# Gated attention: the norm's root moved ahead of evictions on ScalarE; delta net: four fill steps fewer in a head

## What is computed

```python
def gated_deltanet(h, w_in, conv_w, ...):
    proj = h @ w_in                                   # q, k, v, z (the gate), b, a
    qkv = silu(causal_depthwise_conv(proj[..., :3 * DN_WIDTH], conv_w))   # 4 taps
    q, k = l2_normalize(q), l2_normalize(k)           # each head
    o = chunk_gated_delta_rule(q, k, v, beta, g)      # chunks of 64, triangular solve
    o = o * rsqrt(mean(o * o) + EPS) * norm_w * silu(z)
    return o @ w_out

def readout(o_f, o_b, g):                             # the gated linear attention's end
    o = rmsnorm(o_f + flip(o_b), gain)                # mean of squares over a head, its root
    return o * silu(g)
```

## Time and profile before

| | |
|---|---|
| median of three runs | 3222.49 us |
| profiled execution | 3223.74 us |
| its span | 3222.0 us |
| TensorE busy | 3057.1 us, 95% |
| VectorE busy | 1556.7 us, 48% |
| ScalarE busy | 997.9 us, 31% |
| delta net's heads | from about 128 to 745 us |
| gated linear attention | from about 2000 to 2389 us |
| mean granted clock of TensorE | 0.982 |

### The profile page before, as it was taken

How to read it: one execution, slowest core, us unless ns; L and a number is a source line. 1 busy time by engine, 2 the same in 40 slices (tenths; PEclk the granted TensorE clock), 3 DMA queues, 4 the chain that set the end, 5 groups by cost and what they waited for, 6 DMA issues and landing times.

```text
span 3222.0 us, 36124 instructions
## 1 busy us (share of the span) xinstructions
PE 3057.1 (95%) x14927; PEld 2493.4 (77%) x14927; DVE 1556.7 (48%) x1915; ACT 997.9 (31%) x1440; POOL 450.8 (14%) x352
## 2 busy tenths in 40 slices
PE   7899999989899999999979999999998999999997
PEld 5688888878688888888765667888876888888886
DVE  7566666653565553433456773466654222222224
ACT  5555555552211122212333332233232211111111
POOL 4333333321000001001300000233310000000001
PEclk9999999999999999999989999999999999999999
DMA  3111111122133431111220001011131111111111
GB/s 123 40 47 47 46 47 46 47 66 98 59 118 118 128 117 57 47 52 46 92 54 5 9 9 44 20 40 34 53 107 31 52 53 46 46 52 46 46 46 59
DMA packets 77236, 184.76 MB, mean 57 GB/s; under 512 B 7056, under 2 KB 29072, under 8 KB 77072
## 3 DMA queue, kind: packets, MB, share of 16 engines
q1 hardware_dynamic: 77072, 182.44, 17.9%
HBM read 163.87 MB, written 15.79 MB: 56 GB/s over the span
## 4 chain that ended last, share of the span: by engine, by line
PE 85%; DVE 8%; ACT 4%; issue 2%; DMA 0%; POOL 0%; SPq 0%; POOLq 0%; DVEq 0%; ACTq 0%
PE ps L512 38%; PE ps L1561 18%; PE ps L2886 9%; PE ps L2227 4%; DVE b L2835 2%; PE ps L2365 1%; PE ps L2195 1%; PE ps L909 1%; PE ps L2220 1%; PE ps L2219 1%; DVE b L501 1%; ACT b L493 1%; PE ps L916 1%; PE ps L86 1%; PE ps L891 1%
## 5 line engine op out<-in xcount | busy, mean ns | idle before, releaser
L512 PE MATMUL ps<-b 128*128 128x512 f32 x6024 | 1498.5, 400 | 40.1 <-DVE b L501 13.6
L512 PEld LDWEIGHTS ps<-b 128*128 128x128 f32 x6024 | 1111.2, 190 | 258.2 <-issue 19.2
L1561 PE MATMUL ps<-b 128*128 128x512 f32 x2592 | 599.1, 392 | 0.7 <-DVE b L1696 0.7
L1561 PEld LDWEIGHTS ps<-b 128*128 128x128 f32 x2592 | 485.1, 188 | 109.2 <-DVE b L1696 1.1
L501 DVE TENSOR_TENSOR b<-b 128x1024 fp32r<-128x1024 f32 (+1 forms) x206 | 255.4, 1241 | 298.8 <-ACT b L493 291.9
L493 ACT ACTIVATE b<-b 128x1024 fp32r<-128x1024 f32 (+1 forms) x206 | 215.1, 1045 | 524.5 <-PE ps L1561 427.6
L2886 PE MATMUL ps<-b 128*128 128x512 f32 (+1 forms) x1464 | 330.1, 381 | 6.8 <-ACT b L2946 5.9
L2886 PEld LDWEIGHTS ps<-b 128*128 128x128 f32 x1464 | 257.1, 193 | 57.0 <-issue 11.6
L1610 ACT ACTIVATE b<-ps 128x1024 f32<-128x1024 f32 x54 | 55.4, 1026 | 378.4 <-PE ps L512 378.4
L1400 POOL TENSOR_TENSOR b<-b 128x1024 f32<-128x1024 f32 x18 | 43.2, 2399 | 915.5 <-ACT b L1431 915.1
L2227 PE MATMUL ps<-b 128*128 128x512 f32 x320 | 162.9, 592 | 0.0
(11 more groups left out here) (304 smaller groups left out, 3287.9 us busy)
## 6 DMA issues: line engine op xcount, KB each, us to landing
b<-in_down SPq DMA_DIRECT2D x52, 512.0 KB, 3.6
b<-in_mod SPq DMA_DIRECT2D x96, 256.0 KB, 2.6
b<-in_gu SPq DMA_DIRECT2D x44, 512.0 KB, 3.6
b<-scratch SPq DMA_DIRECT2D x38, 512.0 KB, 4.4
b<-in_dn_in SPq DMA_DIRECT2D x32, 512.0 KB, 4.9
b<-in_up SPq DMA_DIRECT2D x32, 512.0 KB, 3.7
b<-in_win SPq DMA_DIRECT2D x26, 512.0 KB, 3.7
scratch<-b SPq DMA_DIRECT2D x18, 512.0 KB, 2.9
```

Of the source, the lines that this page charges most:

```text
L512: ins = e.matmul(ps[:, c], w, h[:, k, c], start=first and k == 0 and i == 0, stop=last and k == KT - 1 and i == 2)
L1561: ins = e.matmul(ps[:, c], w, u[:, at[k], c], start=k == 0 and p == 0, stop=k == n - 1 and p == 2)
```

## The change

In the delta net's half generators of TensorE, ScalarE and VectorE, the number of fill steps behind product "a" becomes 1 + f in levels 1 and 2 only, and 1 in levels 3 to 6. So a head takes four steps fewer, and what of the projections is not done goes on in the next head. In the gated linear attention ScalarE's six fill steps go from ahead of `act_roots` to behind the root.

```diff
@@ pe_delta_half, act_delta_half, dve_delta_half
-            yield 1 + f
+            yield 1 + (f if lv < 3 else 0)
@@ act_gla
             e.activation(B["sq"], B["qf"], ACT.Square).then_inc(*A.up("osq", h))
-            side.fill(self.gla_fill(h, 6))
             self.act_roots(e, A)
             e.wait_ge(*V.at("oms", h))
             e.activation(small[:, 8:16], small[:, 0:8], ACT.Sqrt).then_inc(*A.up("ort", h))
+            side.fill(self.gla_fill(h, 6))
             side.until((h, "g"))
```

## The result

The changed kernel takes 3234.64 us (median of six runs, 3230.99 to 3237.13), the kernel before 3223.12 us beside it (3222.05 to 3225.54): ratio 1.0032, 95% interval 1.0021 to 1.0042. So it is about 11 us slower, where I forecast 13.5 us faster; the time lies outside my range. The profiled execution took 3234.0 us with a span of 3232.2, 10.2 us more than the span before.

What follows compares the result with a forecast made beforehand. TensorE was taken as nearly full in middle heads, idle in the last head and at the attention's root waits. Gains of 11.5 and 3.5 minus 1.5 us made 13.5, so 3222.49 became 3209.0 us; range 3202 to 3216.

Steps and rivals of the forecast that it cites:

- Part 1, the mechanism: Gated attention, first three heads: moving the root ends TensorE's wait of L79 for L2587, 7.6 us, without delaying the evictions.
- Part 1, the size: Gated attention: 7.6 us of waits, 0.5 us for the gate's eviction and 3.4 us of clock, 11.5 us gained, at least 7.6.
- the term for the clock: Gated attention: half-clock stretches right after the first and third heads' stalls vanish, gaining 3.4 us, bounds 0 to 3.4.
- Part 2, heads 0 to 6: Delta net, four fill steps fewer a head: net loss 1.5 us over seven heads, from 2 us gain to 6 us loss.
- That 0.45 us are enough where VectorE is free, and 0.7 us a head is the price where it has taps.: Delta net levels 3 to 6: one short step costs nothing or some 0.1 us; one tap run costs 0.7 us a head.
- That the last two steps are empty.: Delta net: a head has 66 steps but a projection only 64, so the last two were taken as empty.
- That the lag costs nothing but the last head.: Delta net: two steps of lag a head push the last gate's 12 steps, 8.2 us, into head 7; SyncE cost nothing.
- Part 2, the last head: Delta net, head 7: 12.4 us of waits and low clock become 8.9 us, a gain of 3.5 us.
- (a): Last delta-net head, preparation: v's last taps and Silu run there too; 2.0 us of wait, bounds 0 to 3.4.
- (b): Last delta-net head: mixing starts behind the gate's eviction on ScalarE; 5.5 us of wait, bounds 2 to 9, no clock drop.
- (c): Last delta-net head, end: the wait for L1343 is covered, but the sixth tile's piece waits about as much, 1.4 us.
- the one on the other side: Rival, 3%: VectorE bounds the delta net's levels; 28 shortened levels wait 0.68 us each, part 2 costs 18 us, 3229 us.

Runs made afterwards that it cites:

- the root alone: Against the kernel before, only ScalarE's six fill steps in the gated linear attention moved behind the root, delta net unchanged: 3218.69 us, ratio 0.9979.
- the delta net's part alone: Against the kernel before, only the four fill steps fewer a head in levels 3 to 6, attention unchanged: 3239.43 us, ratio 1.0055.
- level 3's kernel: Against the kernel before, one fill step moved from level 3 to the end of the half, so no lag: 3229.69 us, ratio 1.0018.
- the kernel with the gate's unit finished early: Against the kernel before, two steps fewer a head (levels 5 and 6), gate's eviction issued in the projection's last step: 3229.62 us, ratio 1.0018.
- The kernel with full levels and the same lag: Against the changed kernel, the four steps a head taken from the head's end instead of the levels: 3239.94 us, ratio 1.0054 against the kernel before.

## Why the prediction was wrong, point by point

**Part 1, the mechanism: right.** The first attention head's end after the change, ScalarE, VectorE, TensorE:

```profile
2102.96 0.21 ACT L2466 ACTIVATE b<-b 128x8 f32<-128x8 f32 x1 [2.27 <-DVE b L2585]
2103.18 1.28 ACT L2929 ACT_TABLE_LOAD   x1
...
2105.29 1.28 ACT L2929 ACTIVATE b<-ps 128x512 f32<-128x512 f32 x2 [0.82 <-PE ps L2886]
...
2103.20 0.20 DVE L2587 RECIPROCAL b<-b 128x8 f32<-128x8 f32 x1 [0.28 <-ACT b L2466]
2105.77 1.03 PE L79 MATMUL ps<-b 128*128 128x128 f32 x8
```

The root ends 0.2 us behind the mean, the reciprocal 2.4 us ahead of L79, and L79 has no wait. The Silu table is back 0.8 us before the product of the eviction, so the evictions are not late. The three waits' 7.6 us are gone as forecast, and the 0.55 us for the gate's eviction too. This also answers the sentence on the Trainium skill's page "ScalarE: Activation LUTs", section "What ACT_TABLE_LOAD costs": with its drain of about 1380 ns behind the load the eviction would have begun at 2105.8, and it began at 2105.29, when its product came. The row decides.

**Part 1, the size: the term for the clock failed.** I took 3.4 us as a full gain, by the two low stretches directly behind the waits. Those two are gone, but others came: the fourth head had one of 3.4 us, from 2345.1, and now has two, from 2331.5 and 2355.4, and the first 2 us of one of 6.8 from 2392.9. The stage's low clock is 9.1 us in all, and was 10.2. The first three heads went from 100.4, 100.8 and 100.2 us to 96.6, 98.2 and 96.6, a gain of 10.0 us; the missing 1.5 us are two new waits of L2352 for VectorE's L2538, at the ends of the first and the third head, for which I had no term. The fourth head, which the change hardly touches, went from 83.7 to 86.3. In sum 7.4 us for the stage where I had 11.5. And the stage ahead of it, whose code is the same in all kernels, took 417.0 us before, 420.4 after, 420.2 with the root alone, 417.1 with the delta net's part alone. A difference of 3.4 us comes and goes there: in the five traces in which the stage takes 420 us, and in none of the other nine, the low stretch 41 us behind its start is 10.2 us long. So a kernel's clock stretches are worth some 3 us either way to a sum, and I had entered them with one sign.

**Part 2, heads 0 to 6: the step that failed.** I forecast a loss of 1.5 us, at most 6, and it was 18.9. Three parts of it were wrong.
- *That 0.45 us are enough where VectorE is free, and 0.7 us a head is the price where it has taps.* Taken for one level by itself this was right: level 4 costs nothing, and level 3 costs 0.7 us (though GpSimd has a share in that, which I hadn't counted). But I priced one run of taps a head and nothing else. Levels 5 and 6 cost 1.1 us together in the kernel with the gate's unit finished early, with a weight split ahead of the longest wait, and no clock term stood in the sum. In middle heads, four times, waits of 1.4 to 3.4 us are followed by 3.4 or 6.8 us at half clock; a stretch of 3.4 us cost 1.6 us in level 3's kernel, and 1.3 to 1.6 us between two kernels with the same code there. By that the 20.4 us of low clock in the middle heads are an estimated 8 to 10 of the 18.9 us.
- *That the last two steps are empty.* The 65th step evicts the gate, with a table load. Run at the seam of two heads this costs 1.3 us a head. I had counted steps by what TensorE does in them; for ScalarE the step has 2.3 us of work.
- *That the lag costs nothing but the last head.* The kernel with full levels and the same lag lost as much as the whole of part 2, though up to some 4 us of that are waits at its own shortened seam, so the lag's exact price isn't shown. Two steps of lag a head carry every tap, eviction, table load and split to a new place in each head, where I had checked only the queues of SyncE and the third run of taps. By the sixth head L501 stood beside GpSimd's L1252 and L1254, and made the single longest wait.

**Part 2, the last head: nearly right.** The lag of 12 steps, the order at ScalarE and the end came as forecast. (a) For the preparation I took 2.0 us of loss, and its one wait is 0.9 us, for L867. (b) I took 5.5 us for table, Silu, weights and first tile on ScalarE, and TensorE waits 4.9 us for L1043 in all, 3.96 of it in one piece: 1.28 + 1.02 + 1.05 + 1.05 = 4.4 us of work stand ahead. (c) I took 1.4 us for the end, and it is 1.3 for L1331. The miss is the clock: I said none because TensorE is full until then, and it was 0.5 for 6.8 us from inside the wait. The head took 5.6 us more where my terms gave 8.2 - 3.5 = 4.7. I had also read the low stretch before as 6 us, by two windows of it; it is 10.2.

**The rivals.** The one that came is the one on the other side, at 3%: VectorE bounds the levels, 3229 us against 3234.6 measured. Its number is near by luck: it put the whole loss on the levels with a step less, and the runs show a part each from levels, seam, lag and clock. What I held against it, the last head's level with one step and no wait, was a row from a head in which VectorE has no taps to do.

**What stays open.** How the 18.9 us divide exactly between waits and low clock, since each stretch holds waits too, and between the short levels and the lag, which no run has apart in a clean way. Why the clock falls behind some waits and not behind others: in level 3's kernel the same wait of 1.57 us comes in six heads, and the clock falls behind two of them. How much of GpSimd's holding VectorE up is new: its work cut took 7.6 us from heads 4 to 6 together, clock included, but the kernel before was not run with that cut.

## What to carry to other kernels

A step counted as empty must be empty on every engine; read what each of them issues in it before it is taken away. Where engines share one order of steps, a step less moves all that follows: look for the engine that is full at the new place, head by head, in the last as well as in the first. And a step is cheap where the other engine has nothing else to do (level 4) and dear where it has (level 3), so try it level by level rather than by a rule.

## What the runs showed of the hardware that I had not expected

VectorE and GpSimd hold each other up, in the kernel before too: there q's third tap takes 2.32 us beside L1287, against 1.28, and a copy L1154 1.31 to 1.33 us beside L1254 in seven heads, against 0.22. In the changed kernel it is more. L501 takes 1.23 us with GpSimd idle or nearly so and 2.52 us beside L1252; the copy L1154 of 128x128 takes 2.36 us beside L1254, against 0.49 and less with GpSimd's work cut; L1254 itself takes 3.20 us instead of the 2.37 to 2.39 of its seven executions before. In the rows L501 ends about 1.1 us after L1252 has ended (549.65), and L1154 ends 0.1 us after L1254 (552.92), as if each had waited for the other engine's whole instruction. "SBUF — State Buffer", section "Who interferes with whom", of the Trainium skill says so: a copy in a two-port mode, or an instruction with two SBUF inputs, and a GpSimd instruction that reads SBUF lock one another out for a whole instruction. The trace agrees, with these numbers.

Low clock came in stretches of 3.4, 6.8 and 10.2 us in the delta net, and behind short waits of an engine that is 95% busy over the span. The same code in the same stage took 3.4 us more or less from kernel to kernel.
